# Experts of a mixture layer: the gated activation on ScalarE, the gate half of the up weights in other pieces, and new orders on three engines

## What is computed

```
def run_block(args):
    xblk, e = args
    hu = xblk @ w1[e] + b1[e]                    # w1[e]: 1024 x 2048
    x_glu = jnp.minimum(hu[:, :D_FF], 7.0)
    x_lin = jnp.clip(hu[:, D_FF:], -7.0, 7.0)
    act = x_glu * jax.nn.sigmoid(1.702 * x_glu) * (x_lin + 1.0)
    return act @ w2[e] + b2[e]                   # w2[e]: 1024 x 1024
```

## Time and profile before

| what | value |
|---|---|
| three runs | 2712.66, 2713.0, 2710.13 us; median 2712.66 |
| profiled execution, first to last instruction (its span) | 2710.0 us |
| profiled execution on the clock of the runs | not listed apart; the median lies 2.7 us over the span |
| granted clock of TensorE, mean | 0.981 |
| experts | about 877 us to 2682 us, then 28 us of final norm and store |
| DMA | 607.47 MB, 224 GB/s over the span |

### The profile page before, as it was taken

How to read it: one execution, slowest core, us unless ns; L and a number is a source line. 1 busy time by engine, 2 the same in 40 slices (tenths; PEclk the granted TensorE clock), 3 DMA queues, 4 the chain that set the end, 5 groups by cost and what they waited for, 6 DMA issues and landing times.

```text
span 2710.0 us, 46224 instructions
## 1 busy us (share of the span) xinstructions
PE 2578.3 (95%) x16435; PEld 2210.9 (82%) x16436; DVE 2053.8 (76%) x2514; ACT 1444.2 (53%) x1626; POOL 576.0 (21%) x470
## 2 busy tenths in 40 slices
PE   8999988999897999999999999999999999999995
PEld 4897777777786888777887979899989897898885
DVE  5437788545677987999879787866686778978786
ACT  5446656213443764777557465544454546645554
POOL 0035565202124112121212121111121212111111
PEclk9999999999997999999999999999999999999998
DMA  7121111442345997999879797866686779968783
GB/s 292 39 87 37 32 42 58 163 164 98 92 94 174 385 350 233 365 367 361 295 253 364 249 304 265 291 209 209 192 302 216 243 258 313 350 208 295 266 317 134
DMA packets 275157, 607.47 MB, mean 224 GB/s; under 512 B 21836, under 2 KB 53108, under 8 KB 273952
## 3 DMA queue, kind: packets, MB, share of 16 engines
q1 hardware_dynamic: 254720, 562.81, 58.5%
q0 software_dynamic: 20352, 43.51, 7.1%
HBM read 583.27 MB, written 46.97 MB: 233 GB/s over the span
## 4 chain that ended last, share of the span: by engine, by line
PE 36%; issue 11%; DVE 9%; ACT 5%; DMA 4%; DVEq 1%; POOL 1%; ACTq 0%; POOLq 0%
PE e_acc L2665 7%; PE e_acc L2668 7%; PE e_acc L2666 7%; PE e_acc L2638 4%; PE e_acc L2640 4%; PE e_acc L2639 4%; DMA list_now<-lists 4%; DVE e_slot_r L2821 4%; ACT whi L2749 3%; PE e_tb L2613 1%; DVE yo L2905 1%; DVE e_alo L2830 1%; DVE e_glu L2881 1%; ACT e_xhi L2753 1%; ACT e_ahi L2753 1%
## 5 line engine op out<-in xcount | busy, mean ns | idle before, releaser
L2749 ACT ACTIVATE whi<-e_slot 128x2048 fp32r<-128x2048 f32 x296 | 561.0, 1913 | 390.2 <-PE e_acc L2668 327.2
L2821 DVE TENSOR_TENSOR e_slot_r<-e_slot,whi 128x2048 fp32r<-128x2048 f32 x296 | 674.8, 2286 | 106.2 <-ACT whi L2749 106.2
L2665 PE MATMUL e_acc<-e_xhi,whi 128*128 128x256 f32 x1664 | 398.8, 282 | 4.5 <-ACT e_xhi L2753 4.5
L2749 ACT ACTIVATE whi<-slot 128x2048 fp32r<-128x2048 f32 x148 | 283.0, 1912 | 180.5 <-PE e_acc L2640 180.4
L2821 DVE TENSOR_TENSOR slot_r<-slot,whi 128x2048 fp32r<-128x2048 f32 x151 | 344.3, 2282 | 23.6 <-ACT whi L2749 20.9
L2638 PE MATMUL e_acc<-whi,e_ahi 128*128 128x512 f32 x800 | 320.4, 400 | 4.9 <-DVE e_glu L2881 4.9
L2665 PEld LDWEIGHTS e_acc<-e_xhi,whi 128*128 128x128 f32 x1664 | 313.2, 188 | 7.6 <-ACT e_xhi L2753 7.6
L2571 POOL DMA_INDIRECT sum<-yo,e_idx_now x48 | 115.5, 2407 | 953.6 <-issue 509.8
L2640 PE MATMUL e_acc<-whi,e_alo 128*128 128x512 f32 x800 | 313.2, 392 | 0.0
L2639 PE MATMUL e_acc<-e_slot_r,e_ahi 128*128 128x512 f32 x800 | 311.1, 389 | 0.0
L2638 PE MATMUL e_acc<-whi,e_xhi 128*128 128x512 f32 x768 | 303.7, 395 | 1.5 <-DVE e_slot_r L2821 1.2
(11 more groups left out here) (454 smaller groups left out, 5041.5 us busy)
## 6 DMA issues: line engine op xcount, KB each, us to landing
e_slot<-in_w SPq DMA_DIRECT2D x296, 1024.0 KB, 7.4
slot<-in_w SPq DMA_DIRECT2D x151, 1024.0 KB
rv<-in_w_ada SPq DMA_DIRECT2D x32, 512.0 KB, 5.4
slot<-in_w_in SPq DMA_DIRECT2D x9, 1024.0 KB, 9.1
wa<-in_w_ada SPq DMA_DIRECT2D x8, 1024.0 KB, 17.1
slot<-in_w_in SPq DMA_DIRECT2D x12, 512.0 KB, 4.5
xt<-in_x SPq DMA_DIRECT2D x8, 512.0 KB, 14.8
slot<-in_w_out SPq DMA_DIRECT2D x4, 1024.0 KB, 14.4
```

The costliest lines, as they stand in the source:

```text
L2665: pe.matmul(out[:, c, :], whi[i % RING][:, w], xhi[:, kk, :], start=first, stop=False, skip_group_check=True)
L2749: act.activation(whi[i % RING][:], raw[i % PIECES][:], ACT.Copy).then_inc(S["whi_made"], 1)
L2821: v.tensor_tensor(wlo[i % PIECES][:], raw[i % PIECES][:], whi[i % RING][:].bitcast(F32), ALU.subtract).then_inc(S["wlo_made"], 1)
```

## The change

Four things change in `experts`, and one ahead of it.

1. **Activation.** ACT computes x times sigmoid(1.702 x) in one instruction (`Gelu_apprx_sigmoid`) into `e_swish`: in a short unit straight from the accumulator, in a long one from `e_glu`, which DVE still makes with the bias. The clamp of the gate values comes behind it in a short unit, as a minimum with the function's value at 7 (`GLU_MAX`), in DVE's one remaining instruction (L2916 of the changed kernel) with the linear values. L2881 and L2900 are gone.
2. **The + 1** of the linear values moves into the bias row: GpSimd adds it once, on 64 x 1,024 numbers, and ACT's copy of the bias waits for that.
3. **Pieces.** Pieces 0 to 3 are now 2 row tiles by all 1,024 gate columns, and each sums in both `acc[0]` and `acc[1]`; all gate columns are complete after piece 3. The linear halves (4, 5 and 6, 7) go to `acc[2]` and `acc[0]`. PE needs `acc[1]` half a piece into the unit, and waits there for `take(0)` alone (`y_first`); it waits for `take(1)` ahead of piece 4. `take(0)` waits for the first half of piece 11 (`y_half`) instead of all of it.
4. **Orders** of DVE, ACT and PE as the diff shows: `linear(0)` and `idx_next` now come after piece 5 instead of piece 3, `turn_act(0)` after piece 6 instead of 5, `turn_act(1)` ahead of piece 9 instead of in its middle.

The diff, cut to what the text speaks of:

```diff
+GLU_MAX = LIMIT / (1.0 + math.exp(-1.702 * LIMIT))
...
-                    act.wait_ge(S["bias_in"], 16 * 2)
+                    act.wait_ge(S["bias_one"], 1)
...
+            g.wait_ge(S["bias_in"], 16 * 2)
+            g.tensor_scalar(yo[0:2 * NE, 1, :], yo[0:2 * NE, 1, :], 1.0, None, ALU.add).then_inc(S["bias_one"], 1)
...
 def load_piece(sp, dram, keep, raw, i, e):
 
     w = (dram["w1"] if i < 8 else dram["w2"])[0][e, :, :].rearrange("a (k p) n -> p (a k) n", p=P)
-    if i < 8:
-        col = (i // 2 % 2) * D + (i // 4) * 512
+    if 4 <= i < 8:
+        col = D + (i - 4) // 2 * 512
         w = w[:, i % 2 * (KT // 2):(i % 2 + 1) * (KT // 2), col:col + 512]
         to = raw[:].rearrange("p (k n) -> p k n", k=KT // 2)
     else:
-        w = w[:, 2 * (i - 8):2 * (i - 8) + 2, :]
+        w = w[:, 2 * (i % 8):2 * (i % 8) + 2, 0:D]
         to = raw[:].rearrange("p (k n) -> p k n", k=2)
     sp.dma_start(to, w).then_inc(keep["w_in"][i], 16)
...
-        ACC_OF = [0, 1, 2, 0]
-        Y_ACC = [1, 2]
+        GLU_ACC, LIN_ACC, Y_ACC = [0, 1], [2, 0], [1, 2]
...
-                g.wait_ge(S["y_taken"], u * 2 + 2)
+                g.wait_ge(S["y_first"], u + 1)
+                g.wait_ge(S["y_taken"], u + 1)
...
-                    def products(i, b):
...
+                    def by_bank(i):
+
+                        if i >= 4:
+                            hf = (i - 4) // 2
+                            return [(acc[LIN_ACC[hf]], D + hf * 512, [(i % 2 * KH + k, k * 512) for k in range(KH)])]
+                        return [(acc[GLU_ACC[j]], j * 512, [(2 * i + k, k * D + j * 512) for k in range(2)]) for j in range(2)]
+
+                    def products(i):
+
+                        for n, (out, col, at) in enumerate(by_bank(i)):
+                            if i == 0 and n == 1:
+                                pe.wait_ge(S["y_first"], u)
+                            if at[0][0] == 0:
+                                pe.matmul(out[:, 0, :], pick1[:], bias[:, col:col + 512], start=True, stop=False)
+                            if n == 0:
+                                pe.wait_ge(S["wlo_made"], u * PIECES + (i + 1))
+                            for kk, w in at:
+                                w = slice(w, w + 512)
+                                mm = three(out[:, 0, :], xhi, xlo, kk, slice(0, P), whi[i % RING][:, w], wlo[i][:, w], kk == KT - 1)
                         return mm
 
...
                     first_pair()
-                    pe.wait_ge(S["y_taken"], u * 2)
                     up(2)
                     up(3)
+                    pe.wait_ge(S["y_taken"], u)
                     up(4)
                     up(5)
+                    pe.wait_ge(S["swish_made"], u * 2 + 1)
+                    up(6)
                     if nb == 1:
                         turn_act(0)
-                    pe.wait_ge(S["glu_ready"], u * 2 + 1)
-                    up(6)
                     up(7)
                     pe.wait_ge(S["lin_ready"], u * 2 + 1)
-                    pe.wait_ge(S["glu_ready"], u * 2 + 2)
+                    pe.wait_ge(S["swish_made"], u * 2 + 2)
                     pe.wait_ge(S["lo_made"], base + AFTER[nb][ACT_GROUP[nb][0]])
                     down(8)
-                    down(9, (lambda: turn_act(1)) if nb == 1 else None)
+                    if nb == 1:
+                        turn_act(1)
+                    down(9)
...
-                    def sigmoid(hf):
-                        act.wait_ge(S["glu_ready"], u * 2 + (hf + 1))
+                    def swished(hf):
                         act.wait_ge(S["act_ready"], u * 2 + hf)
-                        act.activation(sig[:, 0:nb], glu[:, 0:nb], ACT.Sigmoid, scale=1.702).then_inc(S["sig_made"], 1)
+                        if nb == 2:
+                            act.wait_ge(S["glu_ready"], u * 2 + (hf + 1))
+                            src = glu
+                        else:
+                            act.wait_ge(S["piece_done"], u * PIECES + 4)
+                            src = acc[GLU_ACC[hf]]
+                        act.activation(swish[:, 0:nb], src[:, 0:nb], ACT.Gelu_apprx_sigmoid).then_inc(S["swish_made"], 1)
 
...
-                    high(3, u)
-                    high(4, u)
-                    high(5, u)
-                    sigmoid(0)
-                    high(6, u)
-                    high(7, u)
+                    for i in range(3, 8):
+                        high(i, u)
+                    swished(0)
                     high(8, u)
+                    high(9, u)
+                    swished(1)
                     act_part(0)
-                    high(9, u)
-                    sigmoid(1)
                     high(10, u)
                     high(11, u)
+                    act_part(1)
                     high(12, u)
-                    act_part(1)
                     high(13, u)
                     for r in range(2):
                         part(xhi, r, 0, ROW_GROUP[nb][r])
...
...
+                        if nb == 1:
+                            v.sem_inc(S["glu_ready"], 1)
                             return
+                        v.wait_ge(S["piece_done"], u * PIECES + 4)
+                        v.wait_ge(S["bcol_ready"], u + 1)
+                        v.wait_ge(S["swish_made"], u * 2 + hf)
+                        biased(glu, hf, 0, LIMIT, S["glu_ready"])
 
                     def linear(hf):
...
-                        v.wait_ge(S["piece_done"], u * PIECES + (4 * hf + 4))
+                        v.wait_ge(S["piece_done"], u * PIECES + (2 * hf + 6))
...
                         if nb == 2:
-                            v.scalar_tensor_tensor(l_, l_, 1.0 - LIMIT, glu[:, 0:nb], ALU.max, ALU.mult).then_inc(S["mix_ready"], 1)
+                            v.scalar_tensor_tensor(l_, l_, 1.0 - LIMIT, swish[:, 0:nb], ALU.max, ALU.mult).then_inc(S["act_ready"], 1)
                         else:
-                            v.scalar_tensor_tensor(l_, l_, 1.0, glu[:, 0:nb], ALU.add, ALU.mult).then_inc(S["mix_ready"], 1)
-                        v.wait_ge(S["mix_ready"], n)
-                        v.wait_ge(S["sig_made"], n)
-                        v.tensor_tensor(l_, l_, sig[:, 0:nb], ALU.mult).then_inc(S["act_ready"], 1)
+                            v.scalar_tensor_tensor(l_, swish[:, 0:nb], GLU_MAX, l_, ALU.min, ALU.mult).then_inc(S["act_ready"], 1)
...
                     def take(j):
...
-                        x.then_inc(S["y_taken"], 1)
+                        x.then_inc(S["y_taken" if j else "y_first"], 1)
...
-                    rest(3, u)
-                    rest(4, u)
+                    for i in range(3, 7):
+                        rest(i, u)
                     gated(0)
-                    rest(5, u)
-                    rest(6, u)
+                    rest(7, u)
+                    gated(1)
                     linear(0)
                     for b in range(NB):
                         v.wait_ge(gath[b], u * 16 + 16)
                     v.wait_ge(S["mid_ready"], u + 1)
                     next_index(u * 16 + 16)
-                    rest(7, u)
                     rest(8, u)
                     act_part(0)
-                    gated(1)
                     rest(9, u)
                     linear(1)
                     rest(10, u)
...
                     rest(14, u)
-                    v.wait_ge(S["piece_done"], u * PIECES + PIECES)
+                    v.wait_ge(S["y_half"], u + 1)
                     v.wait_ge(S["const_in"], 16)
                     take(0)
+                    v.wait_ge(S["piece_done"], u * PIECES + PIECES)
                     take(1)
```

More of the change, by code:

```diff
@@ L2426, in experts @@
         xg = keep["xg"]
-        glu, sig = t.sb("e_glu", [P, NB, 512]), t.sb("e_sig", [P, NB, 512])
+        glu, swish = t.sb("e_glu", [P, NB, 512]), t.sb("e_swish", [P, NB, 512])
         lin = t.sb("e_lin", [P, NB, 512])
@@ L2702, in down @@
                                     mm = three(out[:, b, :], ahi, alo, kk, slice(b * P, (b + 1) * P), whi[i % RING][:, w], wlo[i][:, w], kk == KT - 1, kk == 0)
[L2703 to L2704 removed]
+                            if j == 0 and i == PIECES - 1:
+                                mm.then_inc(S["y_half"], 1)
                         mm.then_inc(S["piece_done"], 1)
@@ L2867, in biased @@
                     def biased(to, hf, first, low, ready):
-                        out = by_column(acc[ACC_OF[2 * hf + (first > 0)]])
+                        out = by_column(acc[LIN_ACC[hf] if first else GLU_ACC[hf]])
                         for c in range(4):
```

66 lines of the change are left out of this document (27 added, 39 removed).

## The result

The changed kernel takes 2725.8 us (median of seven, 2723.4 to 2728.0), the kernel before 2713.0 (median of seven): a ratio of 1.0045, with an interval of 1.0032 to 1.0058. It is slower by 0.45%, 2.3 us above the forecast of 2723.5 and inside its range. The profiled execution has a span of 2721.8 us, 11.8 more than before, where the forecast had 11 more; it was the fastest of the seven, 2723.4 us on the clock of the runs.

A forecast was written before the change was run, and what follows sets the result against it. PE alone bounds long units; in short ones DVE is full, but a closed loop sets the new period. Terms 17.4 - 12.6 - 0.4 - 1.3 = +3, clock +8: span 2721, median 2723.5 us; range 2705 to 2736.

The forecast's parts named there:

- The loop: Short units behind short ones: closed loop through PE, ACT and DVE lengthens the period from 36.96 to 38.2 us, +17.4 us.
- PE's floor of 35.9: PE's own work in a short unit: the period of 36.96 us less 1.1 us of waits.
- the forecast wait of 2.3: PE waits 38.2 - 35.9 = 2.3 us for take(0) in the middle of piece 0, once a unit.
- Short units behind long ones: Nine runs of short units behind a long one: start waits go, 0.6 us stays at the end; -1.4 each, -12.6 us.
- the 2.0 us of waits: Start of a short unit between long ones: DVE stands for the list of next tokens; idx_next behind piece 5 removes this.
- Nothing in long units: Long units: PE is full there, so fewer instructions on DVE give nothing.
- The end: Very end of the run: only take(1) follows the last matmul, -1.3 us.
- The clock: PE's new wait, 14 times in short units: 5 of 14 followed by a clock fall costing 1.7 us, +8 us.
- three of five waits of that length: Ahead of the experts: of the five PE waits nearest in length, 2.13 to 2.20 us, three were followed by a fall.
- rival 2: Experts: no fall of the clock at PE's new waits, +3 us, 2716 us; chance 0.26.
- What cost nothing: GpSimd's + 1, ACT's function, 4 KB weight rows, lighter DVE in long units: together 0, bounds -2 to +4 us.
- Rival 1: Short units: loop closes sooner, period 36.8 us, lighter DVE wins, -16, 2696 us; chance 0.12, including a mix with the forecast.

The follow-up runs named there:

- The kernel with the list later: Kernel before, with idx_next (indices from the next tokens' list) made behind the remainder of piece 8 instead of ahead of that of piece 7: 2691.0 us, 0.9923.
- the kernel with waits of 2.4 us: Changed kernel with the old activation (DVE's clamps to e_glu, ACT's sigmoid, second multiply) at the new places: 2751.0 us, 1.0144.

## Why the prediction was right, point by point

- **The loop.** 18.7 + 1.4 + 18.0 + 0.1 = 38.2 us was the sum; 18.76, 1.40, 17.97 up to the end of `take(0)` (1160.10 to 1178.07) and 0.05 were measured, 38.18 in all. Each term came from a row of the kernel before, which had no such wait, because the orders are fixed and DVE's instructions don't change in length. Taking out one remainder, taking out half a piece, and putting work into the wait moved the period by 2.21, 1.40 and 0.
- **PE's floor of 35.9** stood 0.1 too high: 35.81 in the kernel with the activation alone. In the changed kernel 38.18 less the wait of 2.14 is 36.04, so the forecast wait of 2.3 came out as 2.14; what makes PE's stretch 0.2 longer in this kernel no run shows. The 14 units cost 16.2 us instead of 17.4, since three of them had taken 37.10, 37.28 and 37.53 before, and not 36.96.
- **Short units behind long ones.** Forecast -12.6 for nine runs, taken over the short unit and the long one ahead of the next; measured -15.6 + 3.1 = -12.5. The prediction put the 2.0 us of waits down to the list, and that is only in part so. The kernel with the list later gains 18.6 in the same nine units by that alone, but the activation alone gains 12.2 there with the wait for the list left in. Pieces and orders alone, which have no such wait either, take 39.68 behind a long unit, 6.9 us in sum under the kernel before; the other 8.7 of the 15.6 come with the lighter DVE. The long units that follow give 3.1 back, 0.35 each, where 0.6 was forecast.
- **Nothing in long units** was forecast, +0.26 each was measured for the three behind long ones. PE stands 0.33 us instead of 0.25 at the start of such a unit. The other 0.18 are no wait: they come up within the first 96 matmuls, which lie 0.120 us apart instead of 0.118. Why is open; in long units of other kernels with these pieces the period was 69.82 to 70.02.
- **The end.** Forecast -1.3; from the start of the last matmul to the end it is 26.97 us (2694.78 to 2721.75) instead of 28.14 (2681.85 to 2709.99), -1.2. But from the copy of that last unit to its last matmul it was 1.5 longer, as the copy stands earlier against PE's work, so that +0.3 remains from the copy on. The step was right by itself and failed as a term of the sum: a sum of periods taken on DVE can't be mixed with a gain taken from PE's end.
- **The clock.** Forecast 5 falls of 14 at 1.7 us, +8; measured 7 at 1.57, +11.0. The price was read well from the one fall of the earlier trace rows; the share of 5 lay between "three of five waits of that length" and the shortest waits. Three of five alone would have been nearer. The count, which began at 2.1 us, had left out the fall at the wait of 1.66 us. Work in the place of the wait took the falls away and left these 14 periods at 38.19, so rival 2, 2716 us, was what the same wait would cost at a full clock. The Trainium skill, TensorE: Matmul & The Clock Gate, "HAM oscillation", warns only of gaps longer than these; the trace disagrees with that in 7 of 14 units.
- **What cost nothing.** ScalarE's function out of the accumulator took 0.58 us, less than the 0.61 at which it was put. PE never waited for `e_swish`.
- **Rival 1** had the loop close sooner; it closed where the sum had it. That the lighter DVE wins, rival 1's outcome, takes the move of one remainder: with `take(0)` ahead of it the kernel takes 2680.2. Rival 1 had named that remainder of piece 14 as what DVE can't be ahead of; moved behind `take(0)` it was still in time for PE.
- **Not in the prediction**: 3.9 us less ahead of the experts, which stood against 15.7 more in them. It belongs to the profiled execution, not to the change (last section). So the loop and the short units behind long ones were forecast within 1.2 us, but that the span came out at +11.8 against +11 is in part luck: three more us for the clock, 0.8 in long units and 1.6 at the end on the one side, 1.2 in the loop and these 3.9 on the other.

## What to carry to other kernels

Ahead of asking what a change saves on a full engine, look for the closed loops that its waits make: from a wait on one engine, through each hand-over, back to the same wait a period later. Add them up from rows of the trace as it is, since instructions in a fixed order keep their length, and compare the sum with the bound engine's own work; if it is longer, an instruction inside the loop costs its full length and one outside costs nothing, as here, until it has used up the idle time of its own path (0.24 of the multiply in `linear(0)`). Then try the two cheapest cuts, moving one instruction out of the loop on the waiting side and pulling work ahead of the wait on the other, before giving up the change, and test its parts alone: here a part worth -30 us was hidden under one worth +41.

## What the runs showed of the chip

- The clock fell after 7 of 14 waits of PE of 2.14 us and after 8 of 14 in the kernel with waits of 2.4 us (and one of 0.5 in the same unit), and after none of 14 of 1.22 us and none of 14 of 0.75 to 0.98. Each fall cost 1.57 us. In these two kernels with falls the waits were alike within 0.02 us, with the same work ahead of them, and yet half of them had a fall; what decides between two such waits these runs don't show. Nor is a short wait safe by itself: ahead of the experts the clock fell at a wait of 1.66 us in nine of the eleven profiled executions (683.68 in the kernel before), and not at a like one 11 us earlier. A length that was harmless in one stretch holds for that stretch.
- From the start to the first copy of the experts the eleven profiled executions took 875.5 to 881.2 us, with no order in it by what was changed. A single profile can't settle 5 us; the periods of one kind of unit, most of them alike within 0.05 us, can settle 0.1.
- With rows of 4 KB for pieces 0 to 3 the same 607.47 MB went in 236,501 packets instead of 275,157. The landing of a megabyte of the weights in pieces 4 to 11, 7.4 us (median) before and 8.6 after, can't be put down to that: in the kernels with the old pieces it was 7.4 to 10.0. In the experts no engine waited for it.
